# Conditioning products of a two-network kernel: multiplied and summed by VectorE in the feed-forward layers instead of by TensorE

## The reference, cut to what matters

```python
# first network, layer i
x = layer_norm(a * x + 0.5 * (silu(x @ w1) * (x @ w3)) @ w2)      # feed-forward, 1024 -> 2816 -> 1024
x = layer_norm(a * x + token_mixing(x, ...))
x = layer_norm(a * x + 0.5 * (silu(x @ w1b) * (x @ w3b)) @ w2b)
x = layer_norm(a * x + sigmoid(x @ ple_w_gate) * (p @ ple_w_proj))
# second network, layer i
mod_l = silu(c)     @ ada_w[i] + ada_b[i]      # 1024 -> 6144
mod_c = silu(c_ctx) @ ada_w[i] + ada_b[i]
```

## Time and profile before

| | |
|---|---|
| median of 3 runs | 3075.56 us |
| lowest and highest | 3074.17, 3078.39 us |
| span of the profiled execution | 3075.3 us |
| its TensorE busy | 2984.1 us, 97% |
| its VectorE busy | 1734.7 us, 56% |
| its ScalarE busy | 715.3 us, 23% |

### The profile page before, as it was taken

The page is one execution under the profiler, slowest core; times in us unless marked ns, Lnnn a source line. Parts: engine busy times, 40 slices in busy tenths (PEclk is TensorE's granted clock), DMA queues, the critical chain, the costliest instruction groups (busy, mean ns, idle before and its releaser), DMA issues. The chain is left out here.

```text
span 3075.3 us, 53460 instructions
## 1 busy us (share of the span) xinstructions
PE 2984.1 (97%) x23086; PEld 2376.8 (77%) x23086; DVE 1734.7 (56%) x2567; ACT 715.3 (23%) x1371; POOL 77.7 (3%) x105
## 2 busy tenths in 40 slices
PE   8999999999999999999999999989999999999998
PEld 8988775559987998685558985655888887766897
DVE  5554456446556564464546556584333664486666
ACT  2102114222112101223322104282111012254210
POOL 1000000000001000000000000000000000001000
PEclk9999999999999999999999999999999999999999
DMA  8645403237656746313227744102222443231553
GB/s 288 223 175 184 142 30 110 97 110 234 206 183 196 260 164 216 134 60 108 99 83 234 237 141 151 55 1 83 82 82 83 150 154 113 98 122 63 165 165 110
DMA packets 279818, 429.94 MB, mean 140 GB/s; under 512 B 10072, under 2 KB 147776, under 8 KB 279584
## 3 DMA queue, kind: packets, MB, share of 16 engines
q1 hardware_dynamic: 273936, 411.52, 39.5%
q0 software_dynamic: 5024, 13.82, 1.4%
q10 hardware_dynamic: 624, 1.19, 0.1%
HBM read 425.45 MB, written 1.05 MB: 139 GB/s over the span
## 5 line engine op out<-in xcount | busy, mean ns | idle before, releaser
L460 PE MATMUL bank<-arena 64*64 64x64 f32 (+8 forms) x7292 | 740.9, 281 | 23.3 <-DVE arena L2069 4.6
L460 PE MATMUL bank<-xT,ring 128*128 128x128 f32 (+2 forms) x4512 | 725.1, 320 | 10.3 <-DVE arena L852 5.7
L460 PEld LDWEIGHTS bank<-arena 128*128 128x128 f32 (+3 forms) x7292 | 640.6, 161 | 120.1 <-issue 36.6
L460 PEld LDWEIGHTS bank<-xT,ring 128*128 128x128 f32 (+1 forms) x4512 | 657.7, 191 | 71.2 <-issue 10.5
L460 PE MATMUL bank<-ring,xT 128*128 128x512 f32 (+3 forms) x1648 | 577.2, 519 | 2.2 <-DVEq L2086 1.2
L460 PEld LDWEIGHTS bank<-ring,xT 128*128 128x128 f32 (+1 forms) x1648 | 264.0, 182 | 253.5 <-issue 237.0
L460 PE MATMUL bank<-ring,arena 128*128 128x256 f32 (+1 forms) x1584 | 436.9, 427 | 12.4 <-issue 5.3
L460 PEld LDWEIGHTS bank<-ring,arena 128*128 128x128 f32 x1584 | 298.2, 190 | 123.9 <-issue 82.0
L852 DVE TENSOR_TENSOR arena<-arena,bank 128x256 f32<-128x256 f32 (+1 forms) x198 | 92.2, 466 | 395.7 <-PE bank L460 254.7
L763 ACT COPY arena<-bank 128x256 f32<-128x256 f32 (+1 forms) x264 | 107.7, 408 | 747.2 <-PE bank L460 745.9
L812 DVE TENSOR_TENSOR arena<-ring,arena 128x1024 f32<-128x1024 f32 (+1 forms) x216 | 257.1, 1190 | 7.4
(11 more groups left out here) (421 smaller groups left out, 2186.8 us busy)
## 6 DMA issues: line engine op xcount, KB each, us to landing
ring<-in_ffn_w SPq DMA_DIRECT2D x88, 1024.0 KB, 8.0
ring<-in_w_in SPq DMA_DIRECT2D x32, 2048.0 KB, 7.7
ring<-in_ffn_w_in SPq DMA_DIRECT2D x44, 1024.0 KB, 6.5
arena<-in_ada_w SPq DMA_DIRECT2D x20, 2048.0 KB, 13.2
ring<-in_ffn_w SPq DMA_DIRECT2D x16, 2048.0 KB, 7.9
ring<-in_ffn_w_out SPq DMA_DIRECT2D x12, 2048.0 KB, 7.8
ring<-in_hgrn_w_in SPq DMA_DIRECT2D x12, 2048.0 KB, 7.9
ring<-in_ffn_w SPq DMA_DIRECT2D x8, 1536.0 KB, 6.6
```

The source lines that it names most:

```text
L460: return self.e.matmul(o, lhsT, rhs, start=start, stop=stop, skip_group_check=True)
```

## The change

In the feed-forward layers of the first network the products go from TensorE to VectorE. For each tile k of 128 rows VectorE multiplies the 128 x 512 weights by the condition of that row and adds them to a sum of the same size, for both conditions where both are needed (the first 16 blocks), for one else. That takes 16 or 8 steps a block. TensorE then sums over the 128 partitions with a stationary operand that is one column of ones. The steps are spread by a table over three places in each up block from block 2 on, and over two places of the first down half. The weights come in quarters of two tiles, each with a semaphore of its own; SP issues a quarter where its part of the buffer is used up. 17 blocks are done so, 4, 4, 4 and 5 in the four layers; two more than before (7 in all) stay with `pe_ada_product`: the transitions behind the first feed-forwards now have three products instead of two, all through the ring. `ada_rows` has three slots instead of two.

In the first three layers the third and fourth sum are done in the second down half, and the last one is turned behind the down pass: TensorE's `pe_ada_turn` and ScalarE's `act_ada_turn` then stand between the feed-forward and the transition.

```diff
-        IN_TRANSITION = ((2, 0, 1, 0), (2, 0, 0, 0))
-        IN_FFN = (((3, 5, 7, 8, 9), (3, 5, 7, 9)), ((3, 5, 7, 8, 9), (3, 5, 7, 8, 9)))
+        IN_TRANSITION = ((3, 0, 1, 0), (3, 0, 0, 0))
+        FFN_ADA = ((0, 1, 2, 3), (7, 8, 9, 10), (12, 13, 14, 15), (19, 20, 21, 22, 23))
...
+        IN_FIRST_DOWN, IN_SECOND_DOWN = 12, 14
+
+        def steps_in(f, t, slot):
+
+            if f < 4 and 2 <= t < 11:
+                return 1 if slot == 0 and t > 3 and f < 3 else 2
+            return {IN_FIRST_DOWN: 10, IN_SECOND_DOWN: 7}.get(t, 0) if f < 3 and slot == 0 else 0
...
+        def quarter_blocks(f):
+
+            used = [block_of_step(f, last_step(f, n, 2 * q + 1)) for n in FFN_ADA[f] for q in range(4)]
+            return [4] * 4 + [max(4, t + 3) for t in used[:-4]]
+
+        def product_blocks(f):
+
+            return [block_of_step(f, last_step(f, n, KT - 1)) + 1 for n in FFN_ADA[f]]
...
+        def pe_ada_sum(pe, n):
+
+            pe.wait_ge(ada_summed, pe.due(ada_summed))
+            pe.wait_ge(to_act.freed, to_act.next_free())
+            bank = to_act.free_bank()
+            last = ada_streams(n) - 1
+            for s in range(last + 1):
+                for j in range(4):
+                    mm = pe.mm(bank[32 * j:32 * j + 32, 0:P], one_column[:, 1 - s:33 - s],
+                               ada_sum(n, s)[:, j // 2, j % 2 * P:(j % 2 + 1) * P], s == 0, s == last)
+            mm.then_inc(to_act.filled, 1)
+
+        def dve_ada_steps(dve, f, t, slot):
+
+            v = nc.vector
+            for n, k, s in ada_steps(f)[steps_before(f, t, slot):steps_before(f, t, slot) + steps_in(f, t, slot)]:
...
+                w_ = f_ada[:, k].rearrange("p (a n) -> p a n", a=2)
+                total, c = ada_sum(n, s), c_wide[:, k, s:s + 1]
+                if k == 0:
+                    ins = v.tensor_scalar(total, w_, c, None, ALU.mult)
+                else:
+                    ins = v.scalar_tensor_tensor(out=total, in0=w_, scalar=c, in1=total, op0=ALU.mult, op1=ALU.add)
+                done = ada_used if k % 2 and last else dve_step
+                ins.then_inc(done, dve.up(done))
+                dve.wait_ge(done, dve.sent(done))
+                if k == KT - 1 and last:
+                    dve.sem_inc(ada_summed, dve.up(ada_summed))
```

In SP's program, before the load of a block, and in VectorE's block:

```diff
+                    for g, at_block in enumerate(quarter_blocks(f)):
+                        if at_block == t:
+                            n, q, G = FFN_ADA[f][g // 4], g % 4, quarters_before(f) + g
+                            l2, c0 = ada_columns(n)
+                            if G > 3:
+                                eng.wait_ge(ada_used, G - 3)
+                            eng.dma_start(f_ada[:, 2 * q:2 * q + 2], k_rows(a["ada_w_2"][l2], c0, 512)[:, 2 * q:2 * q + 2]
+                                          ).then_inc(ada_quarter_landed[q], 16)
...
+                dve_ada_steps(dve, f, b, 0)
                 dve.wait_ge(products, product_count(f, b, 2))
                 dve.wait_ge(products_kept, 4 * n + 1)
                 combine(0, w.s[:, 0], single[:, 0:w.T])
                 dve_T(dve, f, b + 1)
+                dve_ada_steps(dve, f, b, 1)
                 dve.wait_ge(products, product_count(f, b, 6))
                 dve.wait_ge(products_kept, 4 * n + 3)
                 combine(2, w.s[:, 2], pair[:, 0:w.T])
+                dve_ada_steps(dve, f, b, 2)
                 dve.wait_ge(products_kept, 4 * n + 4)
                 combine(1, w.s[:, 3], single[:, 0:w.T])
```

In the down pass, and behind it:

```diff
+        def pe_ada_down(pe, f, j):
+
+            if j == 1:
+                pe.wait_ge(down_read, 2 * passes_before(f) + 1)
+                pe_ada_sum(pe, FFN_ADA[f][2])
+            if j == 2:
+                pe_ada_turn(pe)
+                pe_ada_sum(pe, FFN_ADA[f][3])
...
-                pe_ffn7(pe, ada[0], last_tile=(lambda: pe_last_tile(pe)) if l else None)
+                pe_ffn7(pe, ada[0], lambda half, j: pe_ada_down(pe, 2 * l, j), last_tile=(lambda: pe_last_tile(pe)) if l else None)
+                pe_ada_turn(pe)
                 pe_transition(pe, l, 0)
...
-                act_ffn7(act, ada[0])
+                act_ffn7(act, ada[0], lambda half: act_ada_down(act))
+                act_ada_turn(act)
```

More of the change, by code:

```diff
@@ L893, in dve_ffn7 @@
                 dve_T(dve, f, t0 + 2)
+                if half == 0:
+                    dve_ada_steps(dve, f, IN_FIRST_DOWN, 0)
                 if more:
@@ L942, in dve_ffn7 @@
                     dve_T(dve, f, t0 + 4)
+                if half == 0:
+                    dve_ada_steps(dve, f, IN_SECOND_DOWN, 0)
                 if more:
@@ L1077, in act_prepare_silu, with act_ln_turn @@
             act.wait_ge(act_step, act.sent(act_step))
-        def act_ln_turn(act, l, n, tt, qs, between=None, product=False, home=False):
+        def act_ln_turn(act, l, n, tt, qs, between=None, product=False):
             for q in qs:
@@ new lines, in ada_sum, with ada_steps @@
+        def ada_sum(n, s):
+            if n % 2:
+                return xT[:, 4 + 2 * s:6 + 2 * s, SEQ:512]
+            return at(F_END + 4096 + 512 * s, 2, 256)
+        IN_FIRST_DOWN, IN_SECOND_DOWN = 12, 14
[3 more added lines that the diff above has]
+            return {IN_FIRST_DOWN: 10, IN_SECOND_DOWN: 7}.get(t, 0) if f < 3 and slot == 0 else 0
+        def ada_steps(f):
+            return [(n, k, s) for n in (FFN_ADA[f] if f < 4 else ()) for k in range(KT) for s in range(ada_streams(n))]
@@ new lines, in steps_before, with block_of_step, last_step, quarters_before @@
+        def steps_before(f, t, slot):
+            done = sum(steps_in(f, t_, i) for t_ in range(17) for i in range(3) if (t_, i) < (t, slot))
+            return min(done, len(ada_steps(f)))
+        def block_of_step(f, i):
+            return next(t for t in range(17) if steps_before(f, t + 1, 0) > i)
+        def last_step(f, n, k):
+            return max(i for i, (n_, k_, _) in enumerate(ada_steps(f)) if (n_, k_) == (n, k))
+        def quarters_before(f):
+            return 4 * sum(len(m) for m in FFN_ADA[:f])
@@ new lines, in quarter_landed @@
+        def quarter_landed(G):
+            return 16 * (G // 4 + 1) + (16 if G % 4 < 3 else 0)
+        def quarter_blocks(f):
[3 more added lines that the diff above has]
+            return [block_of_step(f, last_step(f, n, KT - 1)) + 1 for n in FFN_ADA[f]]
+        for f in range(4):
+            assert steps_before(f, 17, 0) == len(ada_steps(f)) and max(quarter_blocks(f)) < 17
@@ L3064, in pe_ada_turn @@
             bank = to_act.free_bank()
-            pe.turn(bank[:, 0:P], ada_rows[:, pe.ada % 2]).then_inc(to_act.filled, 1)
+            pe.turn(bank[:, 0:P], ada_rows[:, pe.ada % 3]).then_inc(to_act.filled, 1)
             pe.ada += 1
@@ L3077, in with_conditions, with ffn_ada @@
             return between
-        def ffn_ada(marks, product, turn):
+        def ffn_ada(f, product, turn):
+            marks = product_blocks(f)
             def between(b):
@@ L4577, in pool_final_weights @@
         def pool_final_weights(pool):
-            pool.wait_ge(final_norm_landed, pool.due(final_norm_landed, 16))
+            pool.wait_ge(lnp_row_landed, pool.due(lnp_row_landed, 16))
             for tt in range(2):
@@ L4659, in first_act @@
                 act_last_tile(act, l, 1)
-                act_ffn7(act, ada[1], (lambda half: act_parameters(act)) if last else None)
+                act_ffn7(act, ada[1], lambda half: act_parameters(act) if last else act_ada_down(act))
+                if not last:
+                    act_ada_turn(act)
                 if last:
```

104 lines of the change are left out of this document (66 added, 38 removed).

## The result

The changed kernel takes 3080.87 us (median of 20 runs, 3078.55 to 3085.37), the kernel before 3075.61 us (20 runs, 3073.84 to 3078.39): ratio 1.0016, 95% interval 1.001 to 1.0022. So it is 5.3 us slower, where 5.6 us faster was forecast; it lies 0.9 us outside the range. The profiled execution's span is 3078.3 us, 3.0 us above that of before; the execution itself took 3080.11 us, so a time lies some 1.8 us above its span, which the page alone didn't show.

The account below looks back on a forecast made before the run. TensorE, busy 2984.1 of 3075.3 us, was taken as the bound. Terms -35.9 + 9.5 + 0.3 + 2.0 + 13.0 + 2.1 + 3.4 = -5.6 us gave 3070.0 us from 3075.56, range 3060 to 3080.

Parts of the forecast that it names:

- What bounds the kernel, and the products removed: TensorE's row bounds the kernel; in the layers 19 products leave it, -35.9 us, and 17 sums add 9.5 us.
- VectorE's steps ... Cost nothing: In the layers, steps of 0.73 us fit VectorE's 4.32 us of waits a block; only layer 4 costs, 0.3 us.
- New wait: TensorE for the finished sum: TensorE waits for a late sum once in each of the four layers: 3 x 0.4 + 0.8 = 2.0 us.
- Queues: SP's quarter loads and the waits around them cost zero, up to 1 us at the start.
- Two products moved into transitions: In two transitions the third product waits for its load and fillers for evictions: 6.5 us each, 13.0 us.
- The clock: The granted clock falls in the gaps of the two long transitions: 1.7 us each, 3.4 us; bounds 0 and 6 each.
- rival 3: Clock falls in both long transitions and stays down over the fillers: 6 us each, +3.0, 3078.6 us; chance 0.12.
- The turn behind the down pass: In the one-product transition ScalarE's root waits for TensorE's last turn: 2.1 us; hidden in the other two.
- 1: The clock holds in the transitions' gaps: -9.0, 3066.6 us; chance 0.25.
- 2: Third load in time or gap covered: transitions cost 7.5 us, not 13.0, no clock loss; -14.5, 3061.1 us; chance 0.1.
- 4: VectorE becomes the bound, blocks growing from 0.86 us a step; at 1.0 us, +21, 3090 us; chance 0.05.
- 5: Products don't come off TensorE's row; small sums cost the upper end: +2.6, 3078 us; chance 0.05.

Follow-up runs that it names:

- Run 5: Changed kernel, each step after a sum's first working on 16 of 512 columns, with count, order and waits kept: 3070.31 us, ratio 0.9979 to the kernel before.
- run 8: Changed kernel, block 2 of the first three layers keeping two steps, five steps moved to the second down half: 3076.57 us, ratio 1.0001 to the kernel before.
- Run 3: Changed kernel with 20 filler matmuls ahead of the third product in the two long transitions: 3077.09 us, ratio 1.0003 to the kernel before.
- run 9: Changed kernel, the fillers ending a transition waiting for a bank of VectorE's ring instead of ScalarE's: 3075.25 us, ratio 0.9998 to the kernel before.
- run 4: Changed kernel, ScalarE loading its table and taking the first root before copying the last turned product: 3078.29 us, ratio 1.001 to the kernel before.
- run 2: Changed kernel, the third product's weights loaded ahead into the idle f_ada, its product between the two turns: 3069.85 us, ratio 0.9981 to the kernel before.
- run 7: Changed kernel with third product's weights loaded ahead, root before late turn, fillers on VectorE's ring, steps spread anew: 3057.59 us, ratio 0.9946 to the kernel before.
- run 1: Kernel before, with only two products moved from the layers into the two transitions, no sums or VectorE steps: 3092.64 us, ratio 1.0055 to the kernel before.

## Why the prediction was wrong

**What bounds the kernel, and the products removed: right.** Run 5 isolates products less sums in layer 2 at -4.99 us, forecast -5.08. A sum took 0.57 us of the row, forecast 0.62 (timeline of the changed kernel, the sum and what follows it):

```profile
76.90 0.64 PE L477 MATMUL bank<-arena,one_column 128*32 128x128 f32 x16
77.47 1.27 PE L477 MATMUL bank<-xT,ring 128*128 128x128 f32 x9
```

**"VectorE's steps ... Cost nothing": the first step that failed.** I counted "a block from 4 on has five" and never blocks 2 and 3, which have six. And I took the room from one block of layer 1, while the first blocks of layers 2 to 4 have less. There VectorE still applies the last rows of the layer norm, 2.45 us, ahead of the product of the block before. The trace of the kernel before shows it in block 2 of layer 2 (timeline, VectorE):

```profile
721.30 1.22 DVE L1028 SCALAR_TENSOR_TENSOR xtok<-xtok,lnp 128x1024 f32<-128x1024 f32 x1
722.56 1.22 DVE L1031 SCALAR_TENSOR_TENSOR xtok<-lnp,xtok 128x1024 f32<-128x1024 f32 x1
...
730.63 0.42 DVE L852 TENSOR_TENSOR arena<-arena,bank 128x256 f32<-128x256 f32 x1 [0.52 <-PE bank L460]
```

The wait ahead of the third combine is 0.52 us there and not 1.69; with the 1.84 us behind it, 2.4 us were free. With 0.79 us a step (0.752 and the gap) four steps and two of the cheaper first steps (1.0 us) take 4.2. After the change, in layer 3 (timeline, VectorE, and TensorE's wait behind it, in block 3):

```profile
984.25 1.22 DVE L1052 SCALAR_TENSOR_TENSOR xtok<-xtok,lnp 128x1024 f32<-128x1024 f32 x1
...
994.24 1.54 DVE L3153 SCALAR_TENSOR_TENSOR arena<-arena,cst 128x512 f32<-128x512 f32 x2
995.82 0.42 DVE L869 TENSOR_TENSOR arena<-arena,bank 128x256 f32<-128x256 f32 x1
996.27 1.54 DVE L3153 SCALAR_TENSOR_TENSOR arena<-arena,cst 128x512 f32<-128x512 f32 x2
...
998.32 1.94 PE L477 MATMUL bank<-xT,ring 128*128 128x128 f32 x15 [1.25 <-DVE arena L869]
```

The same wait is 1.16 us in layer 2 and 1.42 in layer 4, and in layers 2 and 3 a second one of 0.3 follows at block 4. Six steps alone don't make it: layer 1 has six in blocks 2 and 3 as well, but not these rows. There block 3's first combine comes at 56.19 us, 1.0 later than the 3.83 us into the block of the earlier trace rows, and TensorE goes on without a wait (timeline of the changed kernel):

```profile
49.61 5.53 PE L477 MATMUL bank<-xT,ring 128*128 128x128 f32 x48
```

Runs 5 and 8 show it: thin steps take away 2.8 and 3.0 us in layers 2 and 3 (waits for sums among them), and moving block 2's steps alone takes away 2.2 and 2.4. In the fourth layer the shortage was seen ("0.3 us in all") but not its place. The blocks with six steps, seven of them for 40 steps, don't grow one by one: TensorE waits once for a combine, 1.42 us at block 3 as above, and once for the third sum, 1.43 us. That is 2.9 of the 3.2 us that run 5 took away there, forecast 1.1. Where five steps stand the claim held.

**"New wait: TensorE for the finished sum": right in kind, too small.** 3.1 us in five waits, forecast 2.0 beyond what lies in the gap; the longest, 1.43 us in layer 4, is part of the 3.2 above. The prediction named two signs of being wrong that came true here: a wait for a sum above 1 us, and a block above 12.8 us (block 3 of layer 2 takes 13.9).

**"Queues": right as far as seen.** No wait of TensorE or VectorE for a quarter appears among those that matter.

**"Two products moved into transitions": the mechanism right, the load's term too small.** The order came out as written: two products, one turn, a gap behind SP's load, third product, turn, fillers behind the evictions. The load took 9.2 us from issue to use where 7.9 was taken; the third product began 9.6 us after the first, not 8.5. Why it was slower (five loads of the next stage are issued behind it, and the DMA engines are full, share 1.05 to 1.07) wasn't tried.

**"The clock": the second step that failed.** I took 1.7 us a transition from small matmuls at the lower level. The product alone lost 1.7 (3.65 for 1.96), and the fillers another 1.7 (4.53 for 2.84). So a transition costs 1.1 for the load and 1.7 for the second fall more than forecast: 2.8, and 8.2 + 2.8 = 11.0 is what the table has. The second fall is the term that the sum put at nothing. Run 3 shows that without the idle time the product isn't slow; in run 9, without the 1.53 us behind the evictions, the second fall is gone too. This is rival 3 in its place, but the clock didn't stay down from the third product on: it came back and fell again, and a transition lost 3.4 us and not 6. Alone it would have made -5.6 into -2.2; the load's 1.1 us twice brings it to 0, the layers' 5.4 us to +5.4 (6.4 in layers 2 to 4, by VectorE, less 1.0 in layer 1, by before's late start), and the mix takes 2.4 off: +3.0. To put rival 3 at 0.12 with the second stretch without matmuls in sight was the misjudgement, and no rival held VectorE late in a few blocks only.

**"The turn behind the down pass": right,** 2.1 us, taken away by run 4.

**Rivals.** 1 is refuted by the windows. 2 is what run 2 makes: in time, the transitions cost 3.9 us more than before each, against 3.75 forecast, and no clock. 4 happened in a small form only, in five places (blocks 3 and 4 of layers 2 and 3, block 3 of layer 4), not as a bound. 5 is refuted by the sums' price.

**What stays open.** The first mix is 2.2 us shorter after. Its 450.16 us before is the longest of all traces but run 7's: over the nine runs without that one it takes 447.9 to 449.7 us, and the second mix 448.2 to 452.0, with nothing changed in either. So I don't count the 2.4 us to the change but to the difference between one execution and another; what makes that difference isn't shown. Open are also why the third load took 9.2 us, and why run 2's median lies 4.3 us above its trace.

## What to carry to other kernels

A product taken off the busiest engine pays only if what else must move finds a place whose weights are already there: ask for every moved load which slot frees it and how long TensorE stands still, then price the clock for that gap and for each short gap that follows it. Count steps given to an engine with spare time block by block, the first and the last too, against the due time of each thing queued behind them; a room read from one block (here 4.32 us) hides the blocks that carry one step more and those where the engine still has work of the stage before.

## What the runs showed of the hardware that was not expected

One and the same gap of 1.53 us behind ScalarE's evictions sometimes cost the clock and sometimes not. The fillers behind it took 4.53 and 4.38 us in the two long transitions of the changed kernel, but 4.57 and 2.94 in run 1, 4.38 and 2.94 in run 3, and 2.94 twice in run 2. So run 1 has transitions of 21.1 and of 19.6 us. What else decides, the runs don't show.

The same holds for a gap of 2.57 us behind layer 2. In the changed kernel the clock is 1.00 there. In runs 8 and 9 TensorE waits just as long; windows of 5 us, in run 8:

```profile
905.00:910.00 5.00, 2.44 (x35) 1.85 (x36) 2.87 (x6) 3.78 (x8) 0.00 (x0) 0.87 0.12 16
910.00:915.00 5.00, 5.00 (x54) 3.20 (x47) 1.74 (x5) 3.44 (x8) 0.00 (x0) 0.79 1.02 381
```

That transition took 18.33 us in run 8 and 18.34 in run 9, against 17.62. Whether such gaps also spread a kernel's times isn't shown: 6.8 us over the ten runs of run 2, which has them, and 2.4 over eleven of run 7, which has none, but 4.6 over twenty of the kernel before, which has none either.

A scalar-tensor-tensor whose scalar is a column in memory took 752 ns on 128x512 where the one in the earlier trace rows, whose scalar is a plain number in the code, took 692. The trace of the kernel before held the nearer row, a scalar-tensor-tensor of that size with its scalar in a column: 751 ns (L4572, two of them). At 128x16 the step took 235 ns, so of a step some 0.22 us don't depend on its columns.
